# The first cross attention's query projection as seven block products instead of eight, with GpSimd making the halved weights

## The reference, cut to what matters

```python
def cross_attention(hn, mn, w_xq, w_xkv, w_xo):
    q = (hn @ w_xq).reshape(Bsz, S, N_XHEADS, DH_X)
    kv = mn @ w_xkv
    ...
    s = jnp.einsum('bshd,bmhd->bhsm', q, k).astype(jnp.float32) * (DH_X ** -0.5)
    p = jax.nn.softmax(s, axis=-1).astype(v.dtype)
    o = jnp.einsum('bhsm,bmhd->bshd', p, v).reshape(Bsz, S, D_MODEL)
    return o @ w_xo
...
        hn = rmsnorm(h, norm_x_g[l])
        mn = rmsnorm(mem, norm_mem_g[l])
        h = h + cross_attention(hn, mn, w_xq[l], w_xkv[l], w_xo[l])
        hn = rmsnorm(h, norm_ffn_g[l])
        h = h + conv_glu(hn, w_up[l], conv_f_w[l], conv_f_b[l], w_down[l])
```

## Time and profile before

| what | value |
|---|---|
| median of three runs | 2748.8 us (2746.62 to 2751.62) |
| the profiled execution | 2748.8 us, its span 2747.0 us |
| PE busy | 2690.7 us (98%) |
| PE weight loads busy | 2202.3 us (80%) |
| DVE / ACT / POOL busy | 1782.2 / 1122.8 / 1338.7 us |
| granted TensorE clock | 0.994 of full speed |
| DMA | 291.23 MB, mean 106 GB/s |

### The profile page before, as it was taken

One profiled execution on the slowest core, in us unless ns is written; L12 is line 12 of the kernel. 1 busy time (PEld: TensorE's weight loads), 2 busy tenths in 40 slices (PEclk: granted clock), 3 DMA queues, 4 the chain that ended last, 5 costly groups with the idle time before them and its releaser, 6 DMA issues.

```text
span 2747.0 us, 35390 instructions
## 1 busy us (share of the span) xinstructions
PE 2690.7 (98%) x12702; PEld 2202.3 (80%) x12702; DVE 1782.2 (65%) x2101; ACT 1122.8 (41%) x1862; POOL 1338.7 (49%) x782
## 2 busy tenths in 40 slices
PE   8999999999999999999999999999999999999999
PEld 6888787878778888888887777778887788888886
DVE  7888643345866666976845456884548655557776
ACT  4256623132433333443413525563457333334444
POOL 4323123455689999100466321555165788884002
PEclk9999999999999999999999999999999999999999
DMA  4100324343122222651422110332022443347413
GB/s 155 34 29 31 108 78 152 131 161 115 48 91 72 88 80 80 227 183 32 165 91 95 46 39 24 130 115 92 16 100 92 161 145 125 127 153 268 165 58 138
DMA packets 109866, 291.23 MB, mean 106 GB/s; under 512 B 10032, under 2 KB 20528, under 8 KB 108976
## 3 DMA queue, kind: packets, MB, share of 16 engines
q1 hardware_dynamic: 99488, 256.74, 27.3%
q10 hardware_dynamic: 10256, 32.86, 3.3%
HBM read 230.32 MB, written 59.24 MB: 105 GB/s over the span
## 4 chain that ended last, share of the span: by engine, by line
PE 75%; issue 11%; DVE 6%; POOL 5%; ACT 2%; DMA 1%; ACTq 0%; POOLq 0%; DVEq 0%; SPq 0%
PE products L953 21%; PE others L1448 14%; PE products L1448 12%; PE others L1520 7%; PE products L1520 7%; POOL w_lo L768 2%; PE products L1047 1%; PE others L953 1%; DVE work L2820 1%; POOL w_hi L761 1%; PE products L1076 1%; PE products L1695 1%; DMA w_raw<-wstream 1%; PE products L1359 1%; PE others L1628 1%
## 5 line engine op out<-in xcount | busy, mean ns | idle before, releaser
L953 PE MATMUL products<-act_hi,w_hi 128*128 128x512 f32 x864 | 347.2, 402 | 1.5 <-DVE act_lo L2776 1.3
L761 POOL TENSOR_TENSOR w_hi<-w_raw,small 128x1024 fp32r<-128x1024 f32 x54 | 110.2, 2042 | 480.6 <-PE products L953 297.1
L953 PE MATMUL products<-act_lo,w_hi 128*128 128x512 f32 x864 | 338.0, 391 | 0.0
L953 PE MATMUL products<-act_hi,w_lo 128*128 128x512 f32 x864 | 337.8, 391 | 0.0
L844 POOL TENSOR_TENSOR w_lo<-w_raw,w_hi 128x512 fp32r<-128x512 f32 x200 | 308.7, 1551 | 42.0 <-ACT w_hi L2263 42.0
L953 PEld LDWEIGHTS products<-act_hi,w_hi 128*128 128x128 f32 x864 | 163.3, 189 | 42.3 <-issue 7.3
L2263 ACT ACTIVATE w_hi<-w_raw 128x512 fp32r<-128x512 f32 x240 | 146.2, 626 | 115.8 <-PE products L1448 48.7
L953 PEld LDWEIGHTS products<-act_hi,w_lo 128*128 128x128 f32 x864 | 162.9, 189 | 35.0
L953 PEld LDWEIGHTS products<-act_lo,w_hi 128*128 128x128 f32 x864 | 163.3, 189 | 31.4 <-issue 0.2
L877 POOL TENSOR_TENSOR w_lo<-w_raw,w_hi 128x512 fp32r<-128x512 f32 x8 | 10.3, 1294 | 363.7 <-ACT w_hi L2303 363.7
L768 POOL TENSOR_TENSOR w_lo<-w_raw,w_hi 128x512 fp32r<-128x512 f32 x80 | 126.1, 1597 | 115.8 <-ACT w_hi L2617 115.8
(11 more groups left out here) (626 smaller groups left out, 7338.5 us busy)
## 6 DMA issues: line engine op xcount, KB each, us to landing
w_raw<-wstream SPq DMA_DIRECT2D x155, 512.0 KB, 3.5
w_raw<-wstream SPq DMA_DIRECT2D x168, 256.0 KB, 2.6
work<-wstream SPq DMA_DIRECT2D x52, 512.0 KB, 4.4
parked_sums<-work SPq DMA_DIRECT2D x20, 1024.0 KB, 5.5
parked_hidden<-work SPq DMA_DIRECT2D x40, 512.0 KB, 3.0
raw<-parked_sums SPq DMA_DIRECT2D x28, 512.0 KB, 8.1
raw<-parked_hidden SPq DMA_DIRECT2D x20, 512.0 KB, 6.6
work<-parked_hidden SPq DMA_DIRECT2D x20, 512.0 KB, 7.7
```

Source lines behind the costliest of these rows:

```text
L761: pool.tensor_tensor(w_hi[:, slot, :], w_raw[:, slot, :], zeros, ALU.add)\
L953: last = pe.matmul(out[:, c], a[:, ws, w], x[:, k, c], start=(k == 0 and i == 0), stop=(k == KT - 1 and i == 2))
```

## The change

The query projection is done as seven products of halves. Call the token halves and the feature halves "lower" and "upper". From these, seven pairs of a 512x512 activation factor and a 512x512 weight factor are formed; the last four weight factors and four activation factors are sums and differences. Each pair is worked off in two units, 14 units in all, each of 2 x 4 x 3 = 24 matmuls of 128x512. The units are blocks 41 to 54 of the stream now, so xo1 begins at block 55 (`MORE = 6` shifts the numbers).

What else follows from it:

- Weight sums for w_xq: SP moves four pairs of its blocks into `W[:, 10:14]` (`query_blocks`), GpSimd makes four sums each (`query_weight_sums`, after its last division of out1), SP stores them in `query_sums` (`park_query_sums`) and loads the units from there or from `wstream` (`query_unit`).
- Activation factors: ScalarE and VectorE make them during q1 (`first_queries` of each). The second factor's low part lies in `W[:, 18:20]`, where the pairs for ffn1 come too. SP's `move_block(0)` therefore waits until units 4 and 5 (of "difference") are done.
- The sums 0, 1 and 2 for ffn1 follow the divisions of units 6, 8 and 10.
- The factor `rstd` is turned into one column for each chunk of tokens by eight small matmuls on PE (`root_columns`, after unit 0) and one VectorE instruction, and it goes into the scale of the exponential.
- Scores 0 and 1 stand before units 12 and 13. Chunk 1's scores have another PSUM place.
- VectorE counts `weights_split` itself; the relay is gone. ScalarE and VectorE still divide units 0 and 1, GpSimd divides units 2 to 13.

```diff
-STAGES = [("z1", 17, 17), ("out1", 8, 8), ("k1", 8, 8), ("v1", 8, 2), ("q1", 8, 9), ("xo1", 8, 8),
+STAGES = [("z1", 17, 17), ("out1", 8, 8), ("k1", 8, 8), ("v1", 8, 2), ("q1", 14, 17), ("xo1", 8, 8),
...
+QUERY_STEPS = ("first", "second", "difference", "corner", "lower", "sum", "last")
...
+            def query_blocks(n):
+
+                if n == 0:
+                    sp.wait_ge(s("product_quarters"), 4 * (BLOCK0["out1"] + 3))
+                elif n == 1:
+                    sp.wait_ge(s("mem_sums"), 1)
+                else:
+                    sp.wait_ge(s("parked_moved"), 16 * (n - 1))
+                for m in range(2):
+                    sp.dma_start(query_sums_at(n)[:, m, :], ap["wstream"][q0 + n + 4 * m]).then_inc(s("block_moved"), 16)
+
+            def park_query_sums(n):
+
                 sp.wait_ge(s("parts_summed"), 4 * n + 4)
-                sp.dma_start(parked_sums[n].rearrange("m p t -> p m t"), sums_at["ffn1"]).then_inc(s("parked_moved"), 16)
-
-            q0 = BLOCK0["q1"]
-            loads(18, q0 + 3)
+                sp.dma_start(query_sums[n].rearrange("m p t -> p m t"), query_sums_at(n)).then_inc(s("parked_moved"), 16)
+
+            def query_unit(u):
+
+                kind, i, slot = QUERY_STEPS[u // 2], u % 2, (q0 + u) % 2
+                m = slice(2 * i, 2 * i + 2)
+                if kind in ("first", "second", "corner"):
+                    m = slice(q0 + 2 * i + 4 * (kind == "corner"), q0 + 2 * i + 4 * (kind == "corner") + 2)
+                    source = ap["wstream"][m, :, half_of(kind != "first")]
+                else:
+                    low, k = {"difference": (0, 0), "last": (0, 1), "lower": (1, 0), "sum": (1, 1)}[kind]
+                    source = query_sums[m, low, :, half_of(k)]
+                    if u == 4:
+                        sp.wait_ge(s("parked_moved"), 64)
+                sp.dma_start(by_half(w_raw[:, slot, :]), source.rearrange("e p t -> p e t")).then_inc(s(f"weights_loaded{slot}"), 16)
...
+            loads(18, 22)
+            for b in range(22, q0 + 3):
+                sp.wait_ge(s("weights_split"), b - 1)
+                if b < q0:
+                    load(b, b % 2)
+                else:
+                    query_unit(b - q0)
+                if b in (22, 23):
+                    query_blocks(b - 22)
+                elif b == 26:
+                    for n in range(2):
+                        park_query_sums(n)
+                        query_blocks(n + 2)
+                elif b in (28, 29):
+                    park_query_sums(b - 26)
             for b in range(q0 + 3, f1):
-                at = b - q0
-                if at == 3:
+                at = b - q0 - MORE
+                if b - q0 == 7:
                     move_block(0)
                 sp.wait_ge(s("weights_split"), b - 1)
-                load(b, b % 2)
-                if at in (4, 6, 8):
-                    park_sums((at - 4) // 2)
-                elif at in (5, 7, 9):
-                    move_block((at - 3) // 2)
-                elif at == 11:
+                if at < KT:
+                    query_unit(b - q0)
+                    if b - q0 in (8, 10, 12):
+                        park_sums((b - q0 - 8) // 2)
+                    elif b - q0 in (9, 11, 13):
+                        move_block((b - q0 - 7) // 2)
+                    continue
...
-            def relay(first, end, count0):
-
-                pool.wait_ge(s("weights_split"), first)
-                with pool.Fori(count0, count0 + end - first) as n:
-                    pool.wait_ge(s("kv_low"), n + 1)
-                    pool.sem_inc(s("weights_split"), 1)
-                made_elsewhere[0] += end - first
...
+            for n in range(4):
+                query_weight_sums(n)
             q0 = BLOCK0["q1"]
-            for b in range(q0 + 2, BLOCK0["ffn1"] + 4):
+            made_elsewhere[0] += q0 + 2 - BLOCK0["k1"]
+            pool.wait_ge(s("weights_split"), q0 + 2)
+            for b in range(q0 + 2, BLOCK0["xo1"]):
                 split(b, b // 2, b % 2)
-                for n in {2: (0,), 4: (1,), 6: (2,), 9: range(3, 8), 10: (8,), 12: (9,)}.get(b - q0, ()):
+                for n in {6: (0,), 8: (1,), 10: (2,)}.get(b - q0, ()):
+                    weight_sums(n)
+            for b in range(BLOCK0["xo1"], BLOCK0["ffn1"] + 4):
+                split(b, b // 2, b % 2)
+                for n in {9: range(3, 8), 10: (8,), 12: (9,)}.get(b - q0 - MORE, ()):
...
+                    if x == "1":
+                        pe.wait_ge(s("evacuated"), PROD0["q1"] + (9 if c < 3 else 17))
+                        pe.wait_ge(s("parts_copied"), 16)
...
+                def query_unit(u):
+
+                    b, p, kind, i = BLOCK0["q1"] + u, PROD0["q1"], QUERY_STEPS[u // 2], u % 2
                     pe.wait_ge(s("weights_split"), b + 1)
-                    room(p)
-                    half_part(b, G[:, p % 2, 0:HALF], 0, range(8)).then_inc(s("product_quarters"), 2)
-                    half_part(b, G[:, p % 2, HALF:T], 1, range(4))
+                    high, low = {"first": (lambda k: lower(act_hi, k), lambda k: lower(act_lo, k)),
+                                 "second": (lambda k: lower(act_hi, 4 + k), lambda k: lower(act_lo, 4 + k)),
+                                 "difference": (lambda k: second_hi[:, k, :], lambda k: second_lo[:, k, :]),
+                                 "corner": (lambda k: upper(act_hi, k), lambda k: upper(act_lo, k)),
+                                 "lower": (lambda k: lower(act_hi, k), lambda k: lower(act_lo, k)),
+                                 "sum": (lambda k: lower(act_hi, 4 + k), lambda k: lower(act_lo, 4 + k)),
+                                 "last": (lambda k: upper(act_hi, 4 + k), lambda k: upper(act_lo, 4 + k))}[kind]
+                    chain_, more = kind in ("first", "difference", "lower"), kind in ("difference", "lower", "last")
+                    if u == 1:
+                        pe.wait_ge(*norm("roots", "q1", 1, 1))
+                    elif kind == "second":
+                        pe.wait_ge(s("evacuated"), p + 1)
+                        pe.wait_ge(*operand_count("operand_lo", "q1", KT))
+                    elif kind == "difference":
+                        pe.wait_ge(s("parts_copied"), 2 * i + 2)
+                        pe.wait_ge(s("factor_lo"), 4)
+                    elif kind == "corner":
+                        pe.wait_ge(s("evacuated"), p + 1 + 2 * i + 2)
+                        pe.wait_ge(s("factor_lo"), 8)
+                    elif kind == "lower":
+                        pe.wait_ge(s("parts_copied"), 4 + 2 * i + 2)
+                        pe.wait_ge(s("factor_lo"), 12)
+                    elif kind == "sum":
+                        pe.wait_ge(s("parts_copied"), 8 + 2 * i + 2)
+                        pe.wait_ge(s("factor_lo"), 20)
+                    elif kind == "last":
+                        pe.wait_ge(s("evacuated"), p + 9 + 2 * i + 2)
+                        pe.wait_ge(s("factor_lo"), 16)
...
+                def root_columns():
+
+                    pe.wait_ge(*norm("roots", "q1", 1, 1))
+                    pe.wait_ge(s("evacuated"), PROD0["q1"])
+                    for c in range(NCH):
+                        last = pe.matmul(G[:, 0, c:c + 1], rstd[:, c * CH:(c + 1) * CH], ident[:, 0:1], start=True, stop=True)
+                    last.then_inc(s("token_columns"), 1)
+
+                def first_queries():
+
+                    query_unit(0)
+                    root_columns()
+                    for u in range(1, 12):
+                        query_unit(u)
                     scores(0)
-                    half_part(b, G[:, p % 2, HALF:T], 1, range(4, 8)).then_inc(s("product_quarters"), 2)
+                    query_unit(12)
                     scores(1)
+                    query_unit(13)
...
+                act.wait_ge(s("product_quarters"), 4 * BLOCK0["q1"])
+                act.wait_ge(s("parked_moved"), 64)
+                for k in range(3):
+                    query_scaled(k)
+                query_scaled(3)
+                for k in range(4):
+                    query_factor_high(second_hi[:, k, :], rest_difference[:, k, :], 2 * k + 2)
+                query_copies(lower_of, query_chain, 0, (0, 1), 0)
+                query_copies(lower_of, query_chain, 1, (2, 3), 0)
...
-                   .then_inc(s("kv_low"), 1)
+                   .then_inc(s("weights_split"), 1)
...
+                for k in range(4):
+                    dve.wait_ge(s("factor_hi"), 2 * k + 2)
+                    made(dve.tensor_tensor(rest_sum(k), scaled_upper(k), scaled_first(k), ALU.subtract))
+                    dve.wait_ge(s("factor_made"), 2 * k + 1)
+                    made(dve.scalar_tensor_tensor(rest_difference[:, k, :], upper(W, 4 + k), col("x1", 4 + k), rest_sum(k), ALU.mult, ALU.subtract))
+                    if k == 2:
+                        dve.wait_ge(s("token_columns"), 1)
```

(11 more changed lines are left out.)

234 lines of the change are left out of this document (164 added, 70 removed).

## The result

The changed kernel takes 2775.9 us, the median of 6 runs (2771.1 to 2778.9), and the kernel before, measured beside it, 2749.0 us (6 runs, 2746.6 to 2751.6). The ratio is 1.0096 with a 95% interval of 1.0083 to 1.0109. The change costs 27 us where 11 were forecast: the sign was right, and the time lies outside the range of 2753 to 2769.

The account below looks back on a forecast made before the run. PE, busy 98% of 2747.0 us, was taken as the bound. Terms -10.9 + 1.5 + 2.8 + 1.2 + 9.5 + 8.6 - 2.5 + 0.8 = +11.0 on 2748.8 gave 2759.8, said as 2760 us; range 2753 to 2769.

Parts of the forecast that it names:

- (a): Query projection matmuls: 336 in place of 384, 48 fewer at 0.2275 us each; -10.9 us, called certain.
- (b): Before unit 0's start (T0): queued stores and moves delay load 27, block 27 starts at 396.6 instead of 394.60; +1.5 us.
- (c): Roots, between units 0 and 1: PE waits 2.3 us for `rstd`, plus 0.5 for eight tiny matmuls; +2.8 us.
- (d): Units 2 to 6: small waits for GpSimd and the token columns, later factor pieces early; +1.2 us, between 0 and 3.
- (e): Unit 7 waits for the first ffn1 pair's move, sums and its division, all after unit 5's end; +9.5 us.
- (f): Units 9 and 11 each wait 4.3 us for the next pair's move, sums and division; +8.6 us in all.
- (g): Attention behind q1: the first two PE waits for VectorE should go; -2.5 us, between 0 and -3.5.
- (h): xo1: later ffn1 sums delay the fourth block's division past PE's need; +0.8 us, 0 to 2.
- Queued transfers before T0: Rival: ahead of unit 0's start, stores and moves cost 6 us instead of 1.5, total 2764.5; chance 0.08.
- Contention in full: Rival: GpSimd instructions in units 2 to 9 each lose a VectorE piece of about 0.65 us; adds 8, 2768; chance 0.12.

Follow-up runs that it names:

- all three edits together: Changed kernel with query-sum stores apart, first ffn1 pair moved early, and ScalarE rounding the high parts of units 2 to 13; 2762.9 us, ratio 1.0055.
- the sums one unit sooner: Against the roots one unit later: ffn1 sums behind units 2, 5, 8, 11, not 3, 6, 9, 12; key products before low parts; 2757.4 us.
- the roots one unit later: Against all three edits together plus sums behind units 3, 6, 9, 12: column matmuls after unit 1, in another PSUM bank; 2750.2 us.

## Why the prediction was off

- **(a) held.** At clock 1.00 two units take 10.9 us (the row from 461.60), and the 48 matmuls are gone.
- **(b), "the store is then done at about 387 ... PE starts block 27 at 396.6", failed by a size.** The store was done at 387.6 as said. Load 27 was issued at 388.4 and landed at 394.6, 1.3 us late; the low part and the `act_lo` behind it, beside GpSimd's last query sums, took 2.29 and 1.67 us instead of 1.2 and 0.65, which is 2.1 more. PE started at 400.1, 3.5 us late, and its 24 matmuls of 256 columns took 4.88 us instead of 3.15, mostly at half the clock. Pulling the stores apart won about 2 us of this stretch; VectorE's slow instructions and the slow start stayed.
- **(c) was nearly right in its wait, not in the rest.** The wait for `rstd` is 1.7 (2.3 said); the eight column products took 1.95 us (0.5 said), and unit 1 behind them 1.7 us more than a unit at full clock. No term stood for the clock. This stretch is on the chain, so here it does count, as it does behind block 27: 1.7 us each, 3.4 of the 16 that are missing.
- **(d), "the later factor pieces are ready ten and more microseconds ahead", failed**, and with it the sentence that waits for `work` would prove the prediction wrong. VectorE's timeline in the changed kernel:

```profile
467.92 2.27 DVE L3321 SCALAR_TENSOR_TENSOR work<-work,cols,tmp 128x512 f32<-128x512 f32 x1
470.11 2.89 DVE L3319 SCALAR_TENSOR_TENSOR work<-work,cols 128x512 f32<-128x512 f32 x1
...
478.14 0.75 DVE L3321 SCALAR_TENSOR_TENSOR work<-work,cols,tmp 128x512 f32<-128x512 f32 x1
```

  The last piece began while GpSimd was idle (477.55 to 478.40) and took 0.75 us; beside a division a piece takes 2.3 to 2.9. The one from 467.92 ends at 470.19 and the one from 470.11 at 473.00, each 0.56 us behind the end of the GpSimd instruction that it met (469.63 and 472.44). I had weighed only what VectorE does to GpSimd, not what GpSimd does to VectorE. It made unit 6 wait 4.0 us. In the time these cost nothing by the chain, because GpSimd's work ran on beside them; and where ScalarE made the high parts, this wait went and the one before unit 7 grew by 2.1 us.
- **(e) and (f) had the right mechanism and too small sizes.** The three waits were to be 9.5, 4.3 and 4.3, and were 5.7, 4.4 and 2.9; but PE's units in between were longer, so the waits understate the loss. By starts, the interval to P7 is 2.8 us over its forecast, nearly all from the first sums (7.7 us, 488.72 to 496.40, where the earlier trace rows had 5.14) and the division (5.1 for 4.4). The next is 2.7 over, from a move that took 7.25 us behind the load of a unit, where 5.0 was taken. The last, with no factor pieces beside it, is within 0.4; its move stands behind a load too and took 5.20, so the queue's order alone doesn't give the 7.25, and what else does is open.
- **(g)** gave 3.3 instead of 2.5 us.
- **(h), "+0.8", failed by a size:** 3.8 us. The sums 8 start 30.6 us later than before (638.84 against 608.29), PE's third block 22.2 later (634.73 against 612.53). That difference is 8.4 where 6.0 was forecast: from the sums 3 to the sums 8 it took 75.8 us instead of the 73.4 carried over from before. And the sums 8 took 6.3 us instead of 5.1.

The largest single error is in (b), then (h), the contended first sums and division, and the queued move. "Queued transfers before T0" was a rival with 4.5 us and a chance of 0.08. T0 came as late as it said, but not for its reason alone: by the rows under (b), 1.3 us of the excess is the load, 2.1 is VectorE beside GpSimd and 1.7 the clock. "Contention in full" was a rival with 8 us and 0.12. In its own stretch, unit 6 to unit 9, GpSimd's instructions grew by 3.3 us (2.6 in the first sums, 0.7 in a division); the rest of the contention lay where it had not looked, in the 2.1 us ahead of T0 and the 1.2 us of the sums 8. So both came true in part, in the same execution, and the range was built as if at most one could. The rule of the Trainium skill that was weighed in the prediction ("SBUF — State Buffer", "Who interferes with whom") spoke for the second. The trace agrees with it in the two pieces under (d) and shows more: both engines lose, and GpSimd's first sum took 2.43 us instead of 1.29 among VectorE pieces of about 0.62 us (four in 2.48), so it lost more than one of them.

The forecasts for the later kernels, from all three edits together to the sums one unit sooner, were each 10 to 16 us too low. They took waits away, with the slow matmuls behind them, that came back at another unit.

Why does the best version (the roots one unit later) not beat the kernel before? Its profiled execution can be summed up. It wins the 10.9 us of (a) and 3.1 in the attention. It loses 1.4 at T0 (440.24 against 438.84; it waits 4.9 us there in the key stage, where the kernel before waits 3.0), and 13.5 within q1, where T0 to the end of unit 13 is 96.8 us and fourteen units and two scores at full clock would be 83.3. Of these 13.5, 6.5 are three waits for GpSimd, 1.7 the column products, 4.9 units 4 and 7 at a clock that had fallen behind such waits (8.44 and 7.41 us), and 0.4 I can't place. The balance is 0.9 us slower, and PE does reach xo1's third block 1.0 us later (613.52 against 612.53).

What stays open: how far the clock alone moves the total. Runs of the changed kernel differ by 8 us (2771.1 at a clock of 0.991, 2778.9 at 0.987), and I can't say which stretches make that up. Part of it lies far ahead of the change: over the first 200 us the profiled executions have a clock of 0.95 to 0.97, and PE reaches block 27's wait up to 5.5 us apart.

## What to carry to other kernels

Halve the work of the bound engine in a stage, and every feeder has half the time for each unit: put their work for each unit, at the durations of a stage in which all run at once, beside the new length, before counting the gain. Follow the chain of waits by starts of units, not by the sum of waits: a wait or a slow unit beside a longer chain on another engine costs nothing, and filling it wins nothing. And when two risks hang on the same crowding, put the case that both happen into the range.

## What the runs showed of the hardware

- TensorE's granted clock fell to 0.50 (1.2 GHz) behind pauses of 4.4, 6.6 and 8.8 us, and in part (0.70 over the first 2.2 us of the window) behind 2.2 us, but not behind 1.15 and 3.3 us. In the changed kernel it was 0.67 behind a wait of 1.7 us and the column products. Behind six equal pauses of 4.4 us each block took 1.46 us longer, and the whole pause cost 6.1 us. 23 matmuls of no use in a wait kept it at 1.00, and the unit behind took 5.6 us instead of 8.0.
- GpSimd's low part of 128x1024 took 2.35 us alone and 2.7 to 3.2 beside VectorE's pieces; VectorE's 128x512 piece 0.75 alone and up to 2.89 beside GpSimd.
- A move of 1 MB took 4.5 us on a quiet queue, and 7.25 and 5.20 behind the load of a unit.
